# A 256-token, two-block mixture kernel: the first scale group on VectorE, dummy square roots behind the squares, one residual ahead of two low parts, and a projection that starts block by block

## The reference, cut to what matters

```python
def rmsnorm(x, g):
    xf = x.astype(jnp.float32)
    y = xf * lax.rsqrt(jnp.mean(xf * xf, axis=-1, keepdims=True) + EPS)
    return (y * g.astype(jnp.float32)).astype(x.dtype)

def modulate(x, g, shift, scale):
    return rmsnorm(x, g) * (1 + scale) + shift
...
    sc = jax.nn.silu(c)
    scc = jax.nn.silu(c_ctx)
    for i in range(DEPTH):
...
        m = (sc @ ada_w[i] + ada_b[i]).reshape(-1, N_MOD, D_MODEL)[:, :, None, :]
        mc = (scc @ ada_w[i] + ada_b[i]).reshape(N_MOD, D_MODEL)[:, None, None, :]

        x = x + 0.5 * m[:, 2] * swiglu(modulate(x, norm_g[i, 0], m[:, 0], m[:, 1]),
                                       ffn_w_gate[i, 0], ffn_w_up[i, 0], ffn_w_down[i, 0])
        if ctx_in_needed:
            h = h + 0.5 * mc[2] * swiglu(modulate(h, norm_g[i, 0], mc[0], mc[1]),
                                         ffn_w_gate[i, 0], ffn_w_up[i, 0], ffn_w_down[i, 0])

        u = modulate(x, norm_g[i, 1], m[:, 3], m[:, 4])
        uc = modulate(h, norm_g[i, 1], mc[3], mc[4]) if ctx_in_needed else None
...
```

## Time and profile before

| what | value |
|---|---|
| median of 3 runs | 3194.2 us (3193.96 to 3195.57) |
| the profiled execution, its own time | 3192.8 us |
| its span in the profile | 3191.1 us |
| busy: PE / DVE / ACT / POOL | 84% / 69% / 32% / 24% |
| chain that ended last: PE / DMA / DVE / ACT | 51% / 23% / 15% / 5% |

### The profile page before, as it was taken

The page is one execution under the profiler, slowest core; times in us unless marked ns, Lnnn a source line. Parts: engine busy times, 40 slices in busy tenths (PEclk is TensorE's granted clock), DMA queues, the critical chain, the costliest instruction groups (busy, mean ns, idle before and its releaser), DMA issues.

```text
span 3191.1 us, 37434 instructions
## 1 busy us (share of the span) xinstructions
PE 2668.4 (84%) x13910; PEld 2008.1 (63%) x13910; DVE 2190.7 (69%) x3907; ACT 1034.9 (32%) x2169; POOL 751.9 (24%) x679
## 2 busy tenths in 40 slices
PE   8999998897699989999886788877877778886656
PEld 5999986686589989999765255522544235542212
DVE  3886866636626868768614966688566976689675
ACT  3433332112324343343322243323342233322212
POOL 0000000002300100000001433345343543445553
PEclk9999998998899999999887899978988889899877
DMA  7767952241048959849546999999999999999997
GB/s 283 272 234 267 364 189 95 93 145 40 1 152 309 376 211 342 302 177 356 218 145 265 421 411 412 420 421 421 417 419 420 412 403 414 412 420 422 421 419 326
DMA packets 136871, 977.07 MB, mean 306 GB/s; under 512 B 15501, under 2 KB 15509, under 8 KB 18848
## 3 DMA queue, kind: packets, MB, share of 16 engines
q0 software_dynamic: 90512, 657.04, 50.6%
q1 hardware_dynamic: 45072, 312.26, 25.7%
q10 hardware_dynamic: 1152, 6.04, 0.5%
HBM read 974.22 MB, written 1.06 MB: 306 GB/s over the span
## 4 chain that ended last, share of the span: by engine, by line
PE 51%; DMA 23%; DVE 15%; issue 5%; ACT 5%; POOL 1%; DVEq 0%; ACTq 0%; POOLq 0%
PE psum L619 50%; DMA rows<-in_peer,eidx 22%; DVE rows L2101 2%; DVE arena L1583 1%; DVE yacc L1450 1%; DVE arena L1447 1%; DVE wlow L1447 1%; ACT L1065 1%; PE psum L622 1%; POOL rows L2225 1%; DVE arena L1450 1%; DVE arena L1453 1%; ACT u L1065 1%; DVE rep L1892 1%; ACT dots L1065 0%
## 5 line engine op out<-in xcount | busy, mean ns | idle before, releaser
L619 PE MATMUL psum<-rows,diag 128*128 128x512 f32 x1440 | 810.9, 708 | 335.2 <-ACT diag L1065 328.3
L2225 POOL DMA_INDIRECT rows<-in_peer,eidx x512 | 638.0, 1246 | 933.9 <-PE psum L619 546.2
L2101 DVE CUSTOM_DVE_ANT_0 rows<-rows,h2tok 128x1024 f32<-128x1024 f32 x512 | 626.6, 1225 | 329.9 <-DMA rows<-in_peer,eidx 321.9
L619 PEld LDWEIGHTS psum<-rows,diag 128*128 128x128 f32 x1440 | 301.6, 222 | 774.1 <-ACT diag L1065 473.4
L619 PE MATMUL psum<-u_hi,whigh 128*128 128x256 f32 x1760 | 503.7, 286 | 17.3 <-DVE u_lo L1450 13.9
L619 PE MATMUL psum<-u_lo,whigh 128*128 128x256 f32 x1760 | 500.7, 284 | 0.0
L619 PE MATMUL psum<-u_hi,wlow 128*128 128x256 f32 x1760 | 500.5, 284 | 0.0
L1447 DVE TENSOR_TENSOR wlow<-wring,whigh 128x2048 fp32r<-128x2048 f32 x165 | 377.1, 2288 | 162.9 <-ACT whigh L1065 156.8
L1065 ACT ACTIVATE whigh<-wring 128x2048 fp32r<-128x2048 f32 x165 | 314.1, 1908 | 207.0 <-PE psum L619 133.8
L619 PEld LDWEIGHTS psum<-u_hi,whigh 128*128 128x128 f32 x1760 | 340.0, 193 | 20.4 <-issue 15.0
L619 PEld LDWEIGHTS psum<-u_lo,whigh 128*128 128x128 f32 x1760 | 340.7, 194 | 0.0
(11 more groups left out here) (263 smaller groups left out, 3231.9 us busy)
## 6 DMA issues: line engine op xcount, KB each, us to landing
arena<-in_ada_t POOLq DMA_DIRECT2D x112, 1024.0 KB, 7.0
wring<-in_ffn_w_gate SPq DMA_DIRECT2D x55, 1024.0 KB, 5.7
wring<-in_ffn_w_up SPq DMA_DIRECT2D x55, 1024.0 KB, 6.5
wring<-in_ffn_w_down SPq DMA_DIRECT2D x55, 1024.0 KB, 6.4
wring<-in_w_in SPq DMA_DIRECT2D x32, 1024.0 KB, 8.8
wring<-in_peer_wq SPq DMA_DIRECT2D x32, 1024.0 KB, 9.7
wring<-in_ssd_w_in SPq DMA_DIRECT2D x30, 1024.0 KB, 4.8
wring<-in_w_out SPq DMA_DIRECT2D x16, 1024.0 KB, 9.3
```

Source lines behind the costliest of these rows:

```text
L619: return nc.tensor.matmul(out, lhsT, rhs, start=start, stop=stop, skip_group_check=shared)
L2101: v.tensor_tensor_reduce(out=rows[:, n % SLOTS, 0:D], in0=rows[:, n % SLOTS, 0:D], in1=h2tok[:, t, :], scale=1.0, scalar=0.0, op0=ALU.mult ...
L2225: pool.indirect_dma_start(out=rows[:, n % SLOTS, :], out_offset=None, in_=A[f"peer{u // 2}"], in_offset=bass.IndirectOffsetOnAxis(ap=eidx[ ...
```

## The change

Four edits.

1. The first scale group (group 1) leaves PE. `ada_w0` has 4 tiles, not 8. POOL issues four tiles of `ada_t` (`scale_chunk`), three of them ahead of everything else that it does; DVE multiplies them in `scale_first` (16 passes) and no longer makes the first three low parts first: low(0, 0) stands in `mods_first`, low(0, 1) and low(0, 2) behind norm 0. `crow` (two rows now) is loaded between `xT` and `hT`, and ACT applies Silu to it ahead of `squares(0)`. On PE `norm_sums(1)` moves between the second and third projection tile.
2. `warm_sqrt`: a square root of one column into an unused tile, ahead of the wait for the sums in every norm, in the scan's group norm, and in the first mix.
3. At the end of ffn(2) the residual comes before low(3, 0) and low(3, 1).
4. Tile 0 of proj_ctx waits for one block of u at a time.

```diff
-STAGES = [("ada0", 8), ("ffn0", 33), ("ffn1", 33), ("proj_ctx", 11), ("proj_lat", 21), ("ssd_out", 8), ("ffn2", 33), ("ffn3", 33), ("pool", 1), ("ffn4", 33)]
+STAGES = [("ada0", 4), ("ffn0", 33), ("ffn1", 33), ("proj_ctx", 11), ("proj_lat", 21), ("ssd_out", 8), ("ffn2", 33), ("ffn3", 33), ("pool", 1), ("ffn4", 33)]
 for _name, _count in STAGES:
...
@@ -553,9 +554,8 @@
-            for group in range(2):
-                for i in range(4):
-                    load(A["ada_w0"][4 * group + i])
+            for i in range(4):
+                load(A["ada_w0"][i])
...
@@ -621,20 +621,21 @@
-            def ada_rows(groups):
-                for g in groups:
-                    for i in range(4):
...
+            def first_rows():
+                for i in range(4):
+                    w = tile().rearrange("p (k n) -> p k n", k=2)
+                    for k in range(2):
+                        for half in range(2):
+                            ins = mm(psum[0:2, half, :], silu_c[:, 2 * i + k, 0:2], w[:, k, half * 512:(half + 1) * 512],
+                                     i == 0 and k == 0, i == 3 and k == 1)
+                    ins.then_inc(weights_consumed, 1)
+                    if i == 1:
+                        pe.wait_ge(std_ready, 1)
+                        norm_sums(1)
+                pe.wait_ge(arow_ready, 1)
+                for b in range(KB):
+                    ins = transpose(bank(6, b * 2, 2), arow[:, 0, b * P:(b + 1) * P])
                 ins.then_inc(arow_turned, 1)
...
@@ -713,6 +714,8 @@
                     for k in range(kb):
+                        if stage == "proj_ctx" and i == 0:
+                            pe.wait_ge(u_ready, k + 1)
...
-            ada_rows((0, 1))
-            pe.wait_ge(std_ready, 1)
-            norm_sums(1)
+            first_rows()
...
             norm_sums(2)
-            pe.wait_ge(u_ready, 8)
             for i in range(11):
...
@@ -1065,6 +1065,7 @@
             act.dma_start(xT[:], A["xT"]).then_inc(x_in, 16)
+            act.dma_start(crow[:, 0:2], A["c_rows"][0:2].unsqueeze(0).to_broadcast([P, 2, D])).then_inc(crow_in, 16)
             act.dma_start(hT[:], A["hT"]).then_inc(h_in_sem, 16)
...
-            f(exp_a[:], cols[0:64, COLS["a_log"][0]:COLS["a_log"][0] + 1], ACT.Exp).then_inc(act_step, 1)
+            act.wait_ge(crow_in, 16)
+            f(crow[:, 0:2], crow[:, 0:2], ACT.Silu).then_inc(crow_ready, 1)
...
+            def warm_sqrt():
+                f(warm[:], eps[:, 0:1], ACT.Sqrt)
             def deviation(n):
+                warm_sqrt()
                 if n:
                     act.wait_ge(un_ready, 8 * n - 7)
...
             squares(0)
+            deviation(0)
             squares(1)
-            act.dma_start(crow, A["c_rows"].unsqueeze(0).to_broadcast([P, 3, D])).then_inc(crow_in, 16)
-            deviation(0)
+            f(exp_a[:], cols[0:64, COLS["a_log"][0]:COLS["a_log"][0] + 1], ACT.Exp).then_inc(act_step, 1)
             for t in range(HIGH_RING):
                 high(0, t)
             high_input(0)
             deviation(1)
-            act.wait_ge(crow_in, 16)
-            f(crow, crow, ACT.Silu).then_inc(crow_ready, 1)
...
             f(z[:], xbc[:, 0:XB, :], ACT.Square).then_inc(gsq_ready, 1)
+            warm_sqrt()
             act.wait_ge(gms_ready, 1)
...
+                if g == 0:
+                    warm_sqrt()
                 yield mix_slot(g, 31)
...
@@ -1460,17 +1468,41 @@
+            def scale_first():
+                dve.wait_ge(crow_ready, 1)
+                for i in range(ADA_TURNS):
+                    if i == 3:
+                        dve.wait_ge(std_ready, 1)
+                        tick(v.reciprocal(rstd[:], std[:]))
+                    dve.wait_ge(ada_in[i % ADA_RING], 16 * (i // ADA_RING + 1))
+                    if i:
+                        dve.wait_ge(ada_step, ADA_FREE + i)
+                    for j in range(2):
+                        w = aring[:, i % ADA_RING, j, :]
+                        c = KB + 2 * i + j
+                        v.tensor_tensor_reduce(out=spare[:, j, :], in0=w, in1=crow[:, 1, :], scale=1.0, scalar=0.0,
+                                               op0=ALU.mult, op1=ALU.add, accum_out=modsc[:, c:c + 1])
+                        ins = v.tensor_tensor_reduce(out=w, in0=w, in1=crow[:, 0, :], scale=1.0, scalar=0.0,
+                                                     op0=ALU.mult, op1=ALU.add, accum_out=mods[:, c:c + 1])
+                    ins.then_inc(ada_step, 1)
+            def mods_first():
+                dve.wait_ge(weights_consumed, consumed("ada0", 3))
+                dve.wait_ge(ada_step, ADA_BASE[0])
+                v.tensor_copy(arow[:, 0, :], psum[0:2, 0:2, :].rearrange("p a b -> p (a b)")).then_inc(arow_ready, 1)
+                for m in (mods, modsc):
+                    tick(tt(m[:, KB:2 * KB], m[:, KB:2 * KB], col("ada_b", KB, KB), ALU.add))
+                settle()
+                tick(stt(gscale[:, 0, :], NORMS[0][3], 1.0, NORMS[0][1], ALU.add, ALU.mult))
+                low(0, 0)
+                dve.wait_ge(arow_turned, 1)
...
@@ -1604,9 +1637,9 @@
-                if n in (0, 2):
-                    low(n + 1, 0)
-                    low(n + 1, 1)
+                if n == 0:
+                    low(1, 0)
+                    low(1, 1)
...
+                if n == 2:
+                    low(3, 0)
+                    low(3, 1)
             dve.wait_ge(cols_in, 16)
-            for t in range(3):
-                low(0, t)
-            mods_first((0, 1), 1)
+            scale_first()
+            mods_first()
             norm(0)
+            low(0, 1)
+            low(0, 2)
...
@@ -2157,6 +2194,14 @@
+            def scale_chunk(i):
+                if i >= ADA_RING:
+                    pool.wait_ge(ada_step, ADA_FREE + i - ADA_RING + 1)
+                pool.dma_start(aring[:, i % ADA_RING].rearrange("p a b -> p (a b)"), A["ada_t"][4 + i]).then_inc(ada_in[i % ADA_RING], 16)
+            for i in range(ADA_RING):
+                scale_chunk(i)
             each(g.memset(ones[:], 1.0))
...
+            scale_chunk(ADA_RING)
             conditioning(0)
```

More of the change, by code:

```diff
@@ L81 @@
 ADA_TURNS = 4
-ADA_BASE = [ADA_FREE + ADA_TURNS * sum(count for _, count, _ in ADA[:n]) for n in range(len(ADA) + 1)]
+ADA_BASE = [ADA_FREE + ADA_TURNS + ADA_TURNS * sum(count for _, count, _ in ADA[:n]) for n in range(len(ADA) + 1)]
 COLS = {}
@@ L159, in program @@
         eps = sb("eps", [P, 1])
+        warm = sb("warm", [P, 1])
         silu_c = sb("silu_c", [P, KB, 3])
@@ L1461, in _ @@
             v.memset(hgate[0:1, 0, 0:1], 0.0).then_inc(ada_step, ADA_FREE)
-            def mods_first(groups, n):
-                for g in groups:
-                    dve.wait_ge(weights_consumed, consumed("ada0", 4 * g + 3))
-                    v.tensor_copy(arow[:, g, :], psum[0:2, 2 * g:2 * g + 2, :].rearrange("p a b -> p (a b)")).then_inc(arow_ready, 1)
-                dve.wait_ge(arow_turned, n)
-                lo, hi = KB * groups[0], KB * (groups[-1] + 1)
-                ps = bank(6, 0, 48).rearrange("p (a b) -> p a b", b=2)
-                tick(tt(mod0[:, lo:hi], ps[:, lo:hi, 0], col("ada_b", lo, hi - lo), ALU.add))
-                tt(mod0c[:, lo:hi], ps[:, lo:hi, 1], col("ada_b", lo, hi - lo), ALU.add).then_inc(mods_ready, 1)
+            def scale_first():
[15 more added lines that the diff above has]
+                    ins.then_inc(ada_step, 1)
@@ new lines, in mods_first @@
+            def mods_first():
[8 more added lines that the diff above has]
+                dve.wait_ge(arow_turned, 1)
+                ps = bank(6, 0, 16).rearrange("p (a b) -> p a b", b=2)
+                tick(tt(mod0[:, 0:KB], ps[:, :, 0], col("ada_b", 0, KB), ALU.add))
+                tt(mod0c[:, 0:KB], ps[:, :, 1], col("ada_b", 0, KB), ALU.add).then_inc(mods_ready, 1)
@@ L1516, in norm @@
                     return
-                scaled(n)
+                if n:
+                    scaled(n)
                 if n == 3:
@@ L1570, in ffn @@
                 dve.wait_ge(crow_ready, 1 if n < 2 else 2)
-                uses = [ADA_TURNS * sum(ADA[m][1] > a for m in range(n)) for a in range(7)]
+                uses = [(2, 1, 1, 0, 0, 0, 0)[a] + ADA_TURNS * sum(ADA[m][1] > a for m in range(n)) for a in range(7)]
                 def condition(a, it):
@@ L2292 @@
         "xT": blocks(I["x"]), "hT": blocks(I["ctx"]), "cols": np.ascontiguousarray(cols),
-        "ada_w0": tiles(I["ada_w"][0][:, 0:2 * D], 2, D), "c_rows": np.concatenate([I["c"].reshape(1, D), I["c_ctx"].reshape(1, D), I["c_2"].reshape(1, D)]),
+        "ada_w0": tiles(I["ada_w"][0][:, 0:D], 2, D), "c_rows": np.concatenate([I["c"].reshape(1, D), I["c_ctx"].reshape(1, D), I["c_2"].reshape(1, D)]),
         "ada_t": tiles(ada_rows, 2, D),
```

4 lines of the change are left out of this document (3 added, 1 removed).

## The result

The changed kernel takes 3170.8 us (median of 4 runs, 3169.5 to 3171.2) against 3194.1 (4 runs, 3193.4 to 3195.6): ratio 0.9927 [0.9911, 0.9942], 23.3 us less. The profiled execution takes 3170.7 us with a span of 3168.7, against 3192.8 and 3191.1.

The account below looks back on a forecast made before the run. It took the kernel as mostly PE-bound, later bound by expert-row DMA. Gains 5.0 + 3.8 + 5.4 + 5.1 = 19.3 us gave 3173.5 for the profiled execution, 3174.9 beside the median; 8 in 10 between 3167.5 and 3183.

Parts of the forecast that it names:

- The start: Kernel start through ffn(0): with the first scale group off PE, ffn(0) starts 8.1 us earlier, of which 5.0 stays.
- Norm 2 and the projection: Norm 2 to proj_ctx: table load hidden and PE released by the first block of u; gain 3.8 us, bounds 2.0 and 6.4.
- End of ffn(2): Up to norm 5's reciprocal: residual first and table load hidden, reciprocal then waits for the lows; gain 5.4 us.
- Table loads: Norms 3, 6, 8 and the first mix: four loads of 1.28 us hidden by dummy roots, gain 5.1 us.
- The rival by which a load costs more than its row: Table switches: each hidden load also gives back a drain as long as itself, 7.7 us more, 3167; chance 0.01.
- The start gives nothing: Kernel start: `crow` lands 5 us later than forecast and delays PE; gain only 14.3 us, 3179.9; chance 0.13.
- the dummy does not do what it says: Dummy roots: the table is loaded again for the real root, six loads, 7.7 us given back, 3182.6; chance 0.04.
- The gathers' rival: Last 1460 us: expert-row gathers slow down as their table moved in HBM, 14.6 us per one per cent; chance 0.04.
- more than I say: Clock stays at 2.4 GHz over shorter pauses, or `crow` is undisturbed: gain 24 to 26 us, about 3169; chance 0.08.

Follow-up runs that it names:

- experiment 1: Changed kernel with the old start of the program restored and no dummy roots in norms 0 and 1, other three edits kept; 3175.2 us, ratio 0.9942.
- experiment 5: The changed kernel measured again with no edit; 3166.8 us, ratio 0.9914.
- experiment 8: Changed kernel with x's squares ahead of the wait for `crow` and low(3,1) behind norm 5, together; 3163.9 us, ratio 0.9905.
- Experiments 10: Changed kernel without the dummy square root of norm 3 alone; 3168.0 us, ratio 0.9915.
- experiment 3: Changed kernel with low(3,0) and low(3,1) ahead of the residual at the end of ffn(2), as before; 3168.5 us, ratio 0.9916.
- experiment 7: Changed kernel with low(3,1) moved behind norm 5; 3165.0 us, ratio 0.9905.
- experiment 11: Kernel before the change with only a dummy square root at norm 3 added; 3191.3 us, ratio 0.9984.
- Experiment 2: Changed kernel with all dummy square roots taken out; 3178.1 us, ratio 0.9948.

## Why the prediction was right, point by point

**The start** (forecast 5.0, measured 5.4; by experiment 1, 5.3). `crow` landed at 15.2 (forecast 15.5), Silu ended at 17.1 (17.4), PE started at 17.75 (18.2), ffn(0) at 47.55 (47.9), and SP's next issue came at 56.79 (57). The route held at each step: sums 6.4 at the low level, tiles 3.5, norm 1's sums 3.7, no wait for the fourth chunk; DVE had 4.05 to spare where I had said 3.1. The giving back held too: of 8.5 us at ffn(0)'s start, 3.1 were lost by norm 1's reciprocal. x landed at 7.7 (8), and `crow` 7.4 behind it (7.5). Over the six traces with this start the gain is 5.0 to 7.0 (experiment 1), so the forecast is at its lower end.

**Norm 2 and the projection** (3.8; 4.7). The load is hidden and the first block releases PE, as said: 4.0 ahead of PE's start, within 3.6 to 4.1. The term that was off in size is tile 0's duration: I had put it between 0.9 longer and 0.8 shorter, taken it as unchanged, and it was 0.7 shorter. In experiment 5 it was 0.2 longer, and the whole term 3.8. With the clock at the high level from the start, as in experiments 1, 8 and 10, the whole term is 6.5, just above my bound of 6.4. Which of these a run gets was not foreseen and is not explained; that the one trace of the change gave 4.7 is partly luck.

**End of ffn(2)** (5.4; 4.8). The order of events is as forecast, with the lows as what is late next; experiment 3 splits 3.9 for the order from 0.9 for the dummy, experiment 7 shows the 1.64 that the lows cost.

**Table loads** (5.1 for four; 1.28 each, 5.0 measured). The rival by which a load costs more than its row falls as it was put: with no dummy, the root starts 1.29 behind the load's start, and where it is hidden ACT gives back 1.2 to 1.3. No drain is seen; the Trainium skill, "ScalarE: Activation LUTs", section "What ACT_TABLE_LOAD costs", has 2.66 for each switch, and the measurement decides.

**What failed is a sentence in the sum: "Other table loads", priced at their own duration and nothing for what follows them.** In the first block and the mix PE runs in bursts between pauses, and where a pause was 1.28 shorter the granted clock of a later burst changed. Experiments 10 and 11 show it at norm 3 (1.6 to 2.3 beside the load). In the mix it is a regularity of the traces: all ten traces with the dummy there have 15.7 to 16.3 for the 64 instructions and 8.2 to 8.5 for the 32, the three without have 17.1 and 8.9. Experiment 2 is one of the three, so it is one of the dummies that does it; norm 3's alone does not (experiment 11), and the others were not tried one by one. These two make 4.1 us. Another 2.3 stand beside the loads of norm 6 and the mix's root, and that the dummies cause them is not shown. Experiment 2, without any dummy, has as much or more of them; experiment 1, with all of these dummies, takes 77.5 from norm 8's reciprocal to the mix's root, against 77.3 before and 74.6 with the change. Together the forecast lacked 6.4 us of gain. 3.9 were lost elsewhere, 1.4 in ffn(1), which five of ten traces have, and 2.5 in the gathers; so the span fell by 22.4 and not by 19.3. The median came 4.1 below the forecast, 1 of it the scatter between executions. That the sum came so close is partly luck, since what it lacked on either side cancelled for the most part.

**The rivals.** "The start gives nothing" falls by 15.2 for `crow`; "the dummy does not do what it says" by experiment 2. The gathers' rival is not seen: from the first gather to the end the thirteen traces have 1465.8 to 1472.2 us, before 1466.6, after 1469.1, again 1468.4. The case "more than I say" came half true. The clock stayed high where I had put it, at the projection's start, in three of the nine traces, and the change's repeat in experiment 5 gained 26.9, just past that case's 24 to 26, though its projection was not one of the three. Beyond that it stayed higher after shorter pauses behind norm 3 and in the mix, where I had not looked.

**Left open.** It is open why the state products keep the high level when norm 3's root comes 1.3 us sooner; the traces show only that they do, and pauses of other lengths weren't tried. It is open what decides the level at the projection's start, behind the same pause of 3.56. And it is open whether experiment 8 is really faster than the change by the 3 us of its median. Norm 5's reciprocal is 7.7 earlier than in experiment 5, of which the two edits explain 4.8. Between norm 2's and norm 3's reciprocal, where experiment 8 has no edit of its own, 3.1 are gained, as its projection is one of the three at the high level.

## What to carry to other kernels

Put a one-column activation of the next function in front of a wait for another engine, when the function table must change there: each hides a load of 1.28 us for 0.2. Move what only feeds the next stage (here low parts) behind what the waiting engine needs, and stop moving once the idle time is filled. Where PE works in bursts, read a changed pause together with the clock of the burst behind it. Read edits of a few us between marks of their own stage and not from the total, and in more than one trace, since the clock behind the same pause can differ from one execution to the next.

## What the runs showed of the hardware that was not expected

- Eight products of 512 columns took 5.40 us (three traces) or 3.70 us (ten traces) behind the same idle time of 2.2 us, by whether one load of 1.28 us, some 44 us earlier, was hidden.
- Behind the same pause of PE, 3.56 to 3.57 us, the projection ran at the high level from its first instruction in three traces of nine, and not in the other six: its 17th instruction came 6.6 us behind norm 2's reciprocal, or 8.3 to 9.4.
- In the changed kernel the profile prints PEclk 1.00 for 17.7 to 24.1, but the pace is the low level's: 16 sums in 6.42 us at 17.75 against 3.72 at 31.06.
- Three queues with 1 MB loads took turns from the start, so that ACT's landed 6.9, 7.4 and 7.5 us apart; taking one queue away brought `crow` 3.1 us sooner, and that queue's own first load then took 10.6 us to land.
- A pause of PE of 3.38 us for a weight tile was followed by 6.41 us for eight instructions that take 3.45 otherwise: wait and slower clock together cost 6.3 us, about twice the wait.
